# Gate rows multiplied in the front stage, and weight splits in three steps in the second block's attention

## What is computed

```python
def gdn_project(u, w_in, conv_w, a_log, dt_bias):
    B, T, _ = u.shape
    p = u @ w_in
    qkv = jax.nn.silu(short_conv(p[..., :GDN_QKV_DIM], conv_w))
    z = p[..., GDN_QKV_DIM:GDN_QKV_DIM + GDN_VALUE_DIM]
    ab = p[..., GDN_QKV_DIM + GDN_VALUE_DIM:].astype(jnp.float32).reshape(B, T, N_DIRS, 2, GDN_HEADS)
...
    q = l2norm(heads(q)) * (GDN_HEAD_DIM ** -0.5)
    k = l2norm(heads(k))
...
    g = -jnp.exp(a_log.astype(jnp.float32))[:, None, :, None] * jax.nn.softplus(
        a + dt_bias.astype(jnp.float32)[:, None, :, None])
    beta = jax.nn.sigmoid(b)
...
def even_layer(h, positions, norm_g, w_in, b_forget, qn_a, kn_a, qn_b, kn_b,
               lam_q1, lam_k1, lam_q2, lam_k2, subln_g, w_out, lam_init):
...
    proj = hn @ w_in
...
    oa = diff_attention(qa[..., 0, :], qa[..., 1, :], ka[..., 0, :], ka[..., 1, :],
                        va.reshape(b, s_len, N_HEADS_A, A_V_DIM), lam)
...
    ob = fox_attention(qb, kb, vb.reshape(b, s_len, N_HEADS_B, HEAD_DIM), cum_logf)

    mixed = jnp.concatenate([oa.reshape(b, s_len, A_V_WIDTH), ob.reshape(b, s_len, B_WIDTH)],
                            axis=-1) * jax.nn.silu(z)
    return h + mixed @ w_out
```

## Time and profile before

| | us |
|---|---|
| median of 3 runs | 2422.94 |
| lowest, highest | 2420.47, 2424.94 |
| the profiled execution, own time | 2426.08 |
| its span in the trace | 2424.3 |
| PE busy in it | 2232.2 (92%) |
| DVE, ACT, POOL busy | 1031.2, 624.6, 236.5 |
| granted PE clock, mean | 0.972 |

### The profile page before, as it was taken

One profiled execution on the slowest core, in us unless ns is written; L12 is line 12 of the kernel. 1 busy time (PEld: TensorE's weight loads), 2 busy tenths in 40 slices (PEclk: granted clock), 3 DMA queues, 4 the chain that ended last, 5 costly groups with the idle time before them and its releaser, 6 DMA issues. The chain is left out here.

```text
span 2424.3 us, 31378 instructions
## 1 busy us (share of the span) xinstructions
PE 2232.2 (92%) x12076; PEld 1487.7 (61%) x12076; DVE 1031.2 (43%) x1839; ACT 624.6 (26%) x1304; POOL 236.5 (10%) x285
## 2 busy tenths in 40 slices
PE   3999999889897999999999999997999989999999
PEld 2788678689874434343434343433777778787777
DVE  3579635646653121111111111103764665665555
ACT  4343225343431111010101010100343341323421
POOL 4323246600010000000000000000000000000000
PEclk8999999899997999999999999999999999999999
DMA  6114666654447999999999999997421104332131
GB/s 239 53 52 141 216 208 235 170 152 120 147 149 320 426 427 426 427 428 427 428 428 427 428 428 427 428 427 296 144 85 52 53 35 174 111 104 70 36 139 52
DMA packets 197871, 577.88 MB, mean 238 GB/s; under 512 B 65944, under 2 KB 100737, under 8 KB 147713
## 3 DMA queue, kind: packets, MB, share of 16 engines
q1 hardware_dynamic: 189592, 563.13, 60.0%
q0 software_dynamic: 2496, 8.40, 1.1%
q10 hardware_dynamic: 5673, 4.83, 0.6%
HBM read 543.81 MB, written 32.51 MB: 238 GB/s over the span
## 5 line engine op out<-in xcount | busy, mean ns | idle before, releaser
L1833 PE MATMUL ps_gate_up<-expert_ring,pair_columns 128*64 128x512 f32 x1024 | 457.4, 600 | 42.9 <-DMA expert_ring<-in_moe_w_up_dram 35.6
L1834 PE MATMUL ps_gate_up<-expert_ring,pair_columns 128*64 128x512 f32 x1024 | 458.4, 601 | 0.0
L1833 PEld LDWEIGHTS ps_gate_up<-expert_ring,pair_columns 128*64 128x64 f32 x1024 | 136.3, 138 | 324.1 <-issue 321.6
L120 PE MATMUL second_bank<-stream_high,columns_high 128*128 128x512 f32 x640 | 262.7, 410 | 10.4 <-PEq L92 6.3
L122 PE MATMUL second_bank<-stream_high,columns_low 128*128 128x512 f32 x640 | 253.6, 396 | 0.0
L121 PE MATMUL second_bank<-stream_low,columns_high 128*128 128x512 f32 x640 | 253.3, 396 | 0.0
L2139 DVE TENSOR_TENSOR hidden_tokens<-silu_gate,ps_gate_up 64x512 f32<-64x512 f32 x64 | 42.3, 691 | 493.0 <-ACT silu_gate L2020 492.5
L1820 PE MATMUL ps_down<-expert_ring,hidden_columns 128*64 128x512 f32 x512 | 226.6, 595 | 0.0
L1821 PE MATMUL ps_down<-expert_ring,hidden_columns 128*64 128x512 f32 x512 | 226.6, 595 | 0.0
L120 PEld LDWEIGHTS second_bank<-stream_high,columns_high 128*128 128x128 f32 x640 | 123.1, 192 | 41.9 <-issue 15.3
L1820 PEld LDWEIGHTS ps_down<-expert_ring,hidden_columns 128*64 128x64 f32 x512 | 67.5, 137 | 130.1 <-issue 126.0
(11 more groups left out here) (532 smaller groups left out, 3789.1 us busy)
## 6 DMA issues: line engine op xcount, KB each, us to landing
expert_ring<-in_moe_w_gate_dram SPq DMA_DIRECT2D x128, 1024.0 KB, 25.8
expert_ring<-in_moe_w_up_dram SPq DMA_DIRECT2D x128, 1024.0 KB, 26.3
expert_ring<-in_moe_w_down_dram SPq DMA_DIRECT2D x128, 1024.0 KB, 25.8
win_ring<-in_gdn_w_in_dram SPq DMA_DIRECT2D x16, 1024.0 KB, 8.0
late_mod_ring<-in_w_mod_dram SPq DMA_DIRECT2D x16, 1024.0 KB, 5.5
stream_raw<-in_w_in_even_dram SPq DMA_DIRECT2D x16, 1024.0 KB, 5.5
stream_raw<-in_w_in_odd_dram SPq DMA_DIRECT2D x16, 1024.0 KB, 5.2
stream_raw<-in_w_ple_gate_dram SPq DMA_DIRECT2D x8, 1024.0 KB, 10.3
```

The lines of the kernel that those rows point to most:

```text
L120: nc.tensor.matmul(out, sh, mh, start=start, stop=False)
L1833: mm(psA[LO, c], xe[:, e, k], ex.gate_up[s0][:, j, cols], start=(k == 0), stop=(k == KC - 1))
L1834: last = mm(psA[HI, c], xe[:, e, k], ex.gate_up[s1][:, j, cols], start=(k == 0), stop=(k == KC - 1))
```

## The change

1. **Gate rows.** `front` gets `w_ab`, the ring and a new object `early`. ACT rounds the gate weights and weight tile 0 after its last sine, POOL subtracts, and at the end of its stream PE multiplies the gate rows chunk by chunk, each as soon as the columns of chunk k are split. The gate rows land in `early.rows`, two PSUM banks that the front uses for turned tokens (`psX`) and the projection as `psB`.
2. **Order in the projection.** Gate matmuls and their weight split are gone from it, tile 0 is split already, so the counts of `high` and `low` start one lower and PE starts with tile 0 without a wait. `EarlyParts` fixes the addresses of the split tiles so that both stages share them. In SP's queue `gdn_const` moves behind the ring.
3. **Three steps.** `part` is cut into `part_high` and `part_low`; in the attention loop the high part stands at the chunk with t = 0, and the low part comes in two halves of 1024 elements, at the chunks with t = 1 and t = 2. For items with one map `turn_probs` waits for the exponential, not for DVE's reciprocal; `take` waits for that reciprocal on DVE itself.

```diff
@@ front: SP, POOL, ACT, PE
+                sp.dma_start(wab[:, :, :], dram["gdn_w_in"][0].rearrange("(k p) n -> p k n", p=P)[:, :, 4 * D:]).then_inc(wab_in, 16)
+                for i in range(weights.RING):
+                    dst, src = weights.load(i)
+                    sp.dma_start(dst, src).then_inc(ring_in[i], 16)
                 sp.dma_start(per["gdn_const"][:, :], dram["gdn_const"]).then_inc(fetched, 16)
...
                 rotary.on_gpsimd(pool)
+                pool.wait_ge(gates_high, 1)
+                nc.gpsimd.tensor_tensor(early.gl[:, :, :].bitcast(F32R), wab[:, :, :], early.gh[:, :, :], ALU.subtract).then_inc(gates_low, 1)
+                pool.wait_ge(first_high, 1)
+                nc.gpsimd.tensor_tensor(early.wl[:, 0].bitcast(F32R), weights.tile(0), early.wh[:, 0], ALU.subtract).then_inc(first_low, 1)
...
                 rotary.on_scalar(act)
+                act.wait_ge(wab_in, 16)
+                act.wait_ge(summed, PIECES - len(spare))
+                nc.scalar.activation(early.gh[:, :, :].bitcast(F32R), wab[:, :, :], ACT.Copy).then_inc(gates_high, 1)
+                act.wait_ge(ring_in[0], 16)
+                nc.scalar.activation(early.wh[:, 0].bitcast(F32R), weights.tile(0), ACT.Copy).then_inc(first_high, 1)
...
+                pe.wait_ge(kept, KC)
+                pe.wait_ge(gates_low, 1)
+                for k in range(KC):
+                    pe.wait_ge(low, k + 1)
+                    pe.wait_ge(ctx_low, k + 1)
+                    for out, lo, hi in ((psX[0:GW, 0, :], CTX, N), (psX[0:GW, 1, 0:CTX], 0, CTX)):
+                        split_product(nc, out, [early.gh[:, k], early.gl[:, k]], [u[:, k, lo:hi] for u in U], k == 0, k == KC - 1)
@@ gdn_projection
-                take_low_of(0)
                 take_low_of(1)
...
-                        sp.wait_ge(low, (i - RING + 1) * CB)
+                        sp.wait_ge(low, (i - RING + 1) * CB - 1)
...
-                pe.wait_ge(gates_parted, 2)
-                for out, lo, hi in ((psB[0:2 * DH, 0, :], CTX, N), (psB[0:2 * DH, 1, 0:CTX], 0, CTX)):
-                    for k in range(KC):
-                        last = split_product(nc, out, [gh[:, k], gl[:, k]], [u[:, k, lo:hi] for u in U], k == 0, k == KC - 1)
-                last.then_inc(g_rows, 1)
...
-                        pe.wait_ge(low, n + 1)
+                        if n >= 1:
+                            pe.wait_ge(low, n)
...
-                take_high_of(0)
                 take_high_of(1)
-                act.wait_ge(g_rows, 1)
...
-                take_high(nc, gh[:, :, :], wab[:, :, :]).then_inc(gates_parted, 1)
-                dve.wait_ge(gates_parted, 1)
-                take_low(nc, gl[:, :, :], wab[:, :, :], gh[:, :, :]).then_inc(gates_parted, 1)
@@ WeightStream
+    def part_high(self, dve, g):
         dve.wait_ge(self.loaded[g % self.SLOTS], 16 * (g // self.SLOTS + 1))
         if g >= 2:
             dve.wait_ge(self.used[g % 2], LT * (g // 2))
+        take_high(self.nc, self.high[:, g % 2], self.raw[:, g % self.SLOTS]).then_inc(self.parted, 1)
+
+    def part_low(self, dve, g, rows=slice(0, HK)):
         dve.wait_ge(self.parted, 2 * g + 1)
+        ins = take_low(self.nc, self.low[:, g % 2, rows], self.raw[:, g % self.SLOTS, rows], self.high[:, g % 2, rows])
+        if rows.stop == HK:
+            ins.then_inc(self.parted, 1)
@@ layer_tokens
-                    pe.wait_ge(ready, i + 1)
+                    if MAPS[gi] == 2:
+                        pe.wait_ge(ready, i + 1)
+                    else:
+                        pe.wait_ge(exped, upto(i))
...
                     dve.wait_ge(done, i + 1)
+                    dve.wait_ge(ready, i + 1)
...
                         if t == 0:
-                            stream.part(dve, G0 + g + 1)
+                            stream.part_high(dve, G0 + g + 1)
+                        elif t == 1:
+                            stream.part_low(dve, G0 + g + 1, slice(0, HK // 2))
+                        elif t == 2:
+                            stream.part_low(dve, G0 + g + 1, slice(HK // 2, HK))
```

66 lines of the change are left out of this document (39 added, 27 removed).

## The result

| | us |
|---|---|
| before, median of 4 runs (2420.47 to 2424.94) | 2423.35 |
| changed, median of 4 runs (2394.87 to 2397.26) | 2395.39 |
| ratio, with its 95% interval | 0.9887 (0.987 to 0.9904) |
| span of the profiled execution, before / changed | 2424.3 / 2393.7 |

The changed kernel is 28.0 us faster by the medians and 30.6 us by the two profiled spans. Forecast: 28.9 us.

The account below looks back on a forecast made before the run. The start of the projection was taken as bound by the chain before it, all that follows by PE. Gains of 10.1 + 18.8 = 28.9 us from 2422.9 gave 2394.0 us; forecast band 2390 to 2399, whole range 2388 to 2406.

Parts of the forecast that it names:

- Part 1: Front: gate rows follow DVE chunk by chunk, tile 0 starts at 59.85 instead of 69.96; gain 10.1 us, passed on whole.
- rival A: Front: PE's clock does not hold while waiting between chunks; gain 3.1 to 5.6 us, time 2398.5 to 2401; chance 0.12.
- two scale operations: Front, DVE near 43.4: not held up by POOL's subtraction; by the shared-port rule about 0.7 us later, gain 9.4.
- Rival C: Between front and end: part 1's gain is not passed on, a transfer or stage having its own pace; 2404; chance 0.04.
- Part 2: Attention loops: splitting in three shrinks PE's stalls; gain 18.8 us, bounds 8 and 24.
- Even scores: Even attention loop, scores waiting for the exponential, 6.6 us in 4 waits: gain 4.2 us.
- Odd: Odd attention loop, waits of 8.0 us in 5: 0.70 stays, the others shrink or all but vanish; gain 6.6 us.
- Even transposes: Even attention loop, transposes waiting for the copy, 4.7 us in 4: 1.30 stays, the rest goes; gain 3.4 us.
- Clock: Attention loops: PE's lower-clock stretches behind stalls of 3.26 and 2.82 us and one at 2309 go; gain 5.8 us, otherwise 0.
- Rival B: Attention loops: part 2 yields only 8 us, other waits take over and clock stretches stay; 2404.8 us; chance 0.15.
- D: Attention loops: low halves stall PE and lower its clock, kernel slower; 2435 us with ten clock drops; chance 0.03.
- E: Front and loops: both parts give about nothing, the stalls and tile 0's wait having other causes; 2422 us; chance 0.03.

Follow-up runs that it names:

- v_both_trims: Changed kernel with the last split's pieces and fourth output mix moved to other turns and POOL's tile 0 subtraction halved: 2393.43 us against the changed kernel's 2398.73.
- Front alone: Changed kernel with the attention code of before, the whole split at one place: 2414.34 us against 2425.97 for the kernel before.
- p2_attention_alone: Split in three and wait for the exponential, on the front stage of before: 2407.97 us against 2425.97 for the kernel before.
- g_gate_low_on_dve: Changed kernel with the subtraction for the gates' low part moved from POOL to DVE: 2395.70 us against 2425.97 for the kernel before.

## Why the prediction was right, and where its terms were off

Time 2395.39 against 2394.0, inside the range; the sum of 28.9 us against 28.0 by the medians. Of my signs of being wrong one did show: column scaling starts at 44.33, later than 44 (0.22 us of it is the whole front lying later, 0.44 the held scale operation). The waits in the loops sum to 11.9 us, just under the 12 that I had named, and the even loop is 6.7 us shorter, just under my 7 to 11. The terms:

- **Part 1, 10.1 us forecast.** Measured 9.74 to tile 0. PE follows DVE chunk by chunk, but in this trace it catches up only at the seventh chunk and waits once (0.39 us at 57.78), since the clock rose at 54.2, 5.8 us behind the first gate matmul (taken: 4.9). In the changed kernel's second trace it rose after 2.8 us, and PE waited before the fifth, the sixth and the seventh chunk, the last time here:

```profile
57.98 0.41 PE L120 MATMUL ps_gate_rows<-u_columns_high,w_gates_high 128*32 128x512 f32 x1 [0.39 <-DVE u_columns_low L114]
```

  Tile 0 comes 21.8 us behind the copy in both. So with the overlap the clock's rise no longer sets tile 0's start, which the forecast did not say. The clock stayed at 1.00 across such waits and into tile 0, so rival A is out, and with it, for this place, the oscillation by the Trainium skill (TensorE: Matmul & The Clock Gate, A second HAM failure mode: psum-queue depth-cycling): waits of 0.33 to 0.39 us between chunks did not bring the clock down in any of nine traces. The step that failed is the one on the two scale operations: I let the row of L739 (0.10 us inside POOL's instruction) speak against the Trainium skill's rule of the shared pair of ports. L381 was held for 0.45 us, against 0.7 by the rule's estimate, and removing the overlap gave the 0.45 back (v_both_trims). Why L739 with its 8 elements was not held is open; in the changed kernel the same operation again takes 0.10 us inside a POOL instruction. Rows of another kind could have warned me: DVE's cast of 768 elements takes 0.56 us alone and 0.99 to 1.09 beside POOL's column subtraction.
- **Passed on whole: right.** Front alone gave 11.6 us (7.3 to 13.8 by its interval) against the 9.7 to tile 0. Rival C is out. The 1.3 us in the projection's narrow matmuls were in no term.
- **Part 2, 18.8 us forecast.** 18.0 by the times (p2_attention_alone), 16.3 by the two traces. Even scores: 4.2 forecast, 3.5 measured; the stall behind turn 7 is 0.93 (forecast 0.97). Odd: 6.6 forecast, and 6.2 measured; there the wait of 0.70 that was to stay grew to 1.31, and the others shrank by more than forecast. Even transposes: **3.4 forecast, 0.2 measured; this term failed.** The three waits that I let vanish (2.11, 0.94 and 0.39 us in the kernel before) became 1.24, 0.38 and 0.42, which is 1.4 us gained, and the one that was to stay at 1.30 became 2.43. I took each wait as an insert less slack, and didn't see that at turns 27, 28 and 30 the output mix (1.8 us) follows the piece of split on DVE. At turn 30 the changed kernel puts a low half where there had been none, and the wait of 1.30 that I had set down as "behind the loop and stays" grew to 2.43, by about one low half (1.22 us on DVE). So the new stall is at turn 30 and not after turn 9. The two places that I named for new stalls (1.2 us) show 0.44 and 0.36. What v_both_trims leaves at that place, 0.70 + 0.79 us, is released by ACT's copy again, with no split or mix between the last scores and their maximum.
- **Clock, 5.8 us forecast.** PE's busy time in the loops fell by 6.4 us. The stretches were not the ones that I had listed, though: the kernel before has one that is in none of my rows, behind the stall of 2.0 us,

```profile
1955.30:1958.70 3.40, 3.40 (x13) 0.51 0.00 0
```

  and it went too, while the changed kernel got a new one of the same size (below). The two errors of 1.7 us cancel. And this is the least certain term, since the same stalls are not always followed by the lower clock. The stall of 1.99 us at turn 27, which sits behind ACT's table loads in every trace, has 3.4 us at 0.50 behind it in some executions and none in others. The changed kernel's second trace has it:

```profile
1938.90:1942.30 3.40, 3.40 (x10) 0.50 0.00 0
1959.40:1962.80 3.40, 3.40 (x19) 0.50 0.00 0
```

  There the even loop lasts 130.1 us, in the trace of g_gate_low_on_dve without any lower clock 126.9, and in the three traces with the whole split 135.4. But part of that only moves: the first trace has 3.4 us at 0.50 between the two loops, which the second one hasn't. From the start of the even loop to that of the odd one it is 366.0 to 366.1 us in the three traces with the whole split, 359.3 and 359.1 in the changed kernel's two, and 357.6 in that of g_gate_low_on_dve. So the second part is worth 6.7 to 8.4 us there, depending on the clock, and 8.1 to 9.8 in the odd loop (114.0 to 115.8 us with the whole split, 105.9 to 106.0 changed).
  My ground for taking the stretches as gone, that stalls of 0.89 us leave no lower clock behind, doesn't hold either. In the changed kernel's first trace one begins right behind the waits of 0.69 and 0.89 us with which the even loop starts; it costs 1.7 us, and the other traces don't have it:

```profile
1832.50:1835.90 3.40, 3.40 (x9) 0.50 0.00 0
```

- **Rival B** (8 us) and **D** (slower) are out: the second part alone gave 18.0 us, and 13.3 at the lower end of its interval. **E** (nothing) is out with them.
- The wait for the exponential, costed at nothing, is worth nothing: 0.5 us between the two medians, loops alike.

That the sum came within 1 us has some luck in it: the 3.2 us too much for the even transposes were made up by 1.3 us in the projection, and by waits and clock elsewhere. The profiled spans differ by 30.6 us and not by 28.0, and the changed kernel's profile has the shortest stretch of all between the projection and the even loop.
